# Norms in column form: x turned raw or scaled by its root on TensorE, factor and shift applied per partition

## The chip, the cores and the metric
One NeuronCore of a Trainium2 chip. The metric is the device time of one execution in microseconds (us); the kernel before had a median of 1973.52 us in 3 runs (1971.23 to 1974.72). Engines: PE (TensorE), DVE (VectorE), ACT (ScalarE), POOL (GpSimd), SP (SyncE). All data is fp32.

## The reference, cut to what matters
256 tokens of width 1024. Two transformer blocks, then two blocks that work on two streams, x and y (the context). Every stage begins with an RMS norm, a factor and a shift that depend on the condition c:

```python
h = rms_norm(x, norm1_g[i]) * (1.0 + sc1) + sh1      # rms_norm: x * rsqrt(mean(x*x) + eps) * g
x = x + g1 * attention(h)                            # i = 0 differential, i = 1 stick-breaking
h = rms_norm(x, norm2_g[i]) * (1.0 + sc2) + sh2
x = x + g2 * hierarchical_moe(h)                     # router: h @ w_group, h @ w_expert; 32 experts, top 2
```

The second pair of blocks does the same with one norm ahead of one wide input product. The matmuls contract over the width, so h is needed turned: 128 columns of the width on the partitions, 256 tokens along the row.

## The kernel before, in words
x lies as two tiles of 128 tokens x 1024. Six norms feed x: n = 0 to 3 (two for each of the first blocks, `transpose_h`, `take_hT`, `norm_tile`) and streams p = 1 and p = 3 (`stream_scale`, `stream_shift`, `turn_stream`, `take_turned`); p = 0 and 2 are the context's and stay. At each norm, for both tiles:

- ACT squares a tile with a sum and takes the root (L1436, L1438; L559, L560).
- DVE takes the reciprocal (L1602, L572), multiplies the tile with it and with the row `(1 + sc) * g` in one instruction (L1603, L573) and adds the row `sh` (L1604, L579). The rows hold the same 1024 numbers on all 128 partitions (`rows`), loaded by POOL as 512 KB broadcasts (L1286, L523, L530). In this step the columns are reordered from `(c k)` to `(k c)`, so x and the rows are read with a stride of 8 floats and h is written in order.
- PE turns the 8 chunks of the tile (L1918, L592; one weight load and one matmul each), idles through `keep_warm` matmuls (L584; each is two fp32 passes, so 8 of them are "x16" in the trace) and turns the second tile.
- ACT copies the turned chunks from PSUM to `hT` in four instructions of 512 (L1427). Then the first product starts. Matmuls of fp32 data are two instructions each, almost all recorded at the helper's line L1896.

The order of the work is written out by hand: every engine has its own list and waits on semaphores. PE carries, between its other work, 64 small products of the condition with `ada_w` and `w_mod` (`ada_item`), whose weights POOL loads into three buffers (L1295, `ada_load`); every 8 of them give rows of factors and shifts that DVE adds (L1582) and POOL stores to HBM and loads back when needed (`norm_load`, `norm_rows`). The large weights run on SP's queue through a ring of six 2 MB slots (L1230, L1251, L1254), a slot being loaded again when PE has used it.

For n = 0 the condition product comes first (eight 1 MB pieces of `ada_w`, t = 0 to 7, two `keep_warm` after each of t = 2 to 6), then its row is added (L1588), spread over partitions by PE (4 products with ones), and only then the norm is taken. After the norm n = 1 or 3 come the router's products, DVE's router chain (L1662 to L1723), the gathers of tokens for the first four experts, and the experts, each waiting for its weights. ACT's list in layer 1 has the context's squares (L559, once its load L1379 has landed, which POOL issues when h is done) between `take_hT(3)` and the two exponentials of the router.

Of the kernel before, what the change touches and what calls it, by code (L numbers as in the profile page):

```python
# [25 lines left out]
P = 128  # L26
# [34 lines left out]
COUNT.update({n: (4, 4, 4, 4) for n in ("h2T_mm", "h2T")})  # L61
# [71 lines left out]
def program(nc, a, out, sb, sem, ctx):  # L133
# [79 lines left out]
    lvec = small[:, 32:36]  # L213

# [115 lines left out]
    TURN = ((0, 1, 2, 3), (4, 5, 6, 0))  # L330
# [231 lines left out]
    def gain2(dve, link, p):  # L562

        dve.wait_ge(sem("rows2_in"), 16 * (3, 5, 8, 10)[p])
        link(nc.vector.scalar_tensor_tensor(rows[:, 0, :], rows[:, 0, :], 1.0, rows[:, 2, :], ALU.add, ALU.mult))

    def stream_scale(dve, link, p, t):
# [6 lines left out]
                                            rs2[:, k:k + 1], by_chunk(rows[:, 0, :]), ALU.mult, ALU.mult))  # L574

# [10 lines left out]
    def turn_stream(pe, p, ts, banks, spare=0, idle=(0, 0)):  # L586

        for i in range(TT):
            keep_warm(spare, idle[i])
            pe.wait_ge(sem("h2"), nth("h2", p, i + 1))  # L590
            for t in ts:
                ins = nc.tensor.transpose(bank[banks[(t - ts[0]) // 2]][:, (t % 2 * TT + i) * P:(t % 2 * TT + i + 1) * P],  # L592
                                          h2[p % 2][:, i, t * P:(t + 1) * P], ident)
                if i and t % 2:
                    ins.then_inc(sem("h2T_mm"), 1)

    def take_turned(act, copy, p, ts, banks):

        for t in ts[::2]:
            act.wait_ge(sem("h2T_mm"), nth("h2T_mm", p, t // 2 + 1))  # L600
            copy(hT2[:, t:t + 2, :], bank[banks[(t - ts[0]) // 2]].rearrange("p (t n) -> p t n", t=2)).then_inc(sem("h2T"), 1)

    def fill_mm(mm, p, n, halves, b):
# [112 lines left out]
    def act_second(act, link, copy):  # L716
# [115 lines left out]
        take_turned(act, copy, 3, range(KT), (0, 2, 4, 5))  # L832
# [17 lines left out]
    def dve_second(dve, link):  # L850
# [158 lines left out]
    def pe_second(pe, mm):  # L1009
# [163 lines left out]
        turn_stream(pe, 1, range(KT), (2, 3, 4, 5), 0, (22, 4))  # L1173
        pe.wait_ge(sem("h2T"), every("h2T", 1))
# [25 lines left out]
        turn_stream(pe, 3, range(KT), (0, 2, 4, 5), 3, (0, 13))  # L1200
        pe.wait_ge(sem("h2T"), every("h2T", 3))
# [14 lines left out]
    def _(sp):  # L1216
# [5 lines left out]
        def weight(l, n):  # L1222
# [3 lines left out]
            if n < 6:  # L1226
                src = W[:, n * 512:(n + 1) * 512].rearrange("(p t) n -> p t n", t=KT)
# [56 lines left out]
    def _(pool):  # L1284
# [34 lines left out]
        def norm_load(n):  # L1319
# [27 lines left out]
        row_load(3, a["norm1_g"][0:1, :].to_broadcast((P, D)), "norm_in")  # L1347
# [3 lines left out]
        pool.wait_ge(sem("first_mm"), 4)  # L1351
# [73 lines left out]
    def _(act):  # L1425
# [51 lines left out]
        def take_gathered(l, c, b):  # L1477

            act.wait_ge(sem("gat_mm"), EACH["gat_mm"] * l + c + 1)
            i = c % QUAD  # L1480
            copy(hS[:, c // QUAD % 2, 2 * i:2 * i + 2, 0:QUAD * LIST],
                 bank[b].rearrange("p (t n) -> p t n", t=2)[:, :, 0:QUAD * LIST]).then_inc(sem("hS"), 1)
# [8 lines left out]
        def overflow(l):  # L1491

            o_pe, o_act_done = sem(f"over_pe{l}"), sem(f"over_act{l}")
            for step in range(NX * NOVER):
                act.wait_ge(o_pe, 5 * step + 1)
                copy(o_selT.rearrange("p t n -> p (t n)"), bank[2][:, 0:S]).then_inc(o_act_done, 1)
                copy(o_h.rearrange("p t n -> p (t n)"), bank[4]).then_inc(o_act_done, 1)
# [41 lines left out]
        for l in range(2):  # L1539
# [18 lines left out]
            take_hT(2 * l + 1)  # L1558
# [15 lines left out]
    def _(dve):  # L1574
# [8 lines left out]

        def first_norm():

            dve.wait_ge(free(3), 1)
            dve.wait_ge(sem("first_bias"), 16)
            V.tensor_tensor(line, bank[7], line, ALU.add).then_inc(sem("first_line"), 1)  # L1588
            dve.wait_ge(sem("norm_in"), 16)
            dve.wait_ge(sem("first_mm"), 2)  # L1590
            link(V.scalar_tensor_tensor(rows[:, 0, :], psum[:, 4:6, :].rearrange("p b n -> p (b n)"), 1.0, rows[:, 3, :],
                                        ALU.add, ALU.mult))
            dve.wait_ge(sem("first_mm"), 4)
            for t in range(TT):
                norm_tile(0, t, psum[:, 6:8, :].rearrange("p b n -> p (b n)"))

        def norm_tile(n, t, shift):

            by_chunk = lambda r: r.rearrange("p (c k) -> p k c", k=KT)
            h_ = h[:, t, :].rearrange("p (k c) -> p k c", k=KT)  # L1600
            dve.wait_ge(sem("rms"), TT * n + t + 1)
            link(V.reciprocal(rstd[:, t:t + 1], ss[:, t:t + 1]))  # L1602
            link(V.scalar_tensor_tensor(h_, by_chunk(x[:, t, :]), rstd[:, t:t + 1], by_chunk(rows[:, 0, :]), ALU.mult, ALU.mult))  # L1603
# [650 lines left out]
```

## Time and profile before
| | before |
|---|---|
| median of 3 runs | 1973.52 us |
| profiled execution: its own time / its span | 1969.06 / 1967.2 us |
| granted clock of PE, mean | 0.962 |
| busy: PE / DVE / ACT / POOL | 1747.5 / 467.5 / 360.6 / 93.2 us |
| chain that ended last, by engine | PE 56%, DMA 29%, DVE 8%, ACT 3% |
| HBM read | 580.17 MB |

A busy PE is 89% of the span, `keep_warm` included (59.2 us of it). "Idle before, releaser" says how long an engine stood still ahead of an instruction and whose event ended that. A wait counts only where it lies on the chain that ends last.

### The profile page before, as it was taken

The numbers are of one execution on the slowest core, as the hardware profiler recorded it, in microseconds if no ns is written. First come the engines' busy times: TensorE is split into PE (matmuls) and PEld (weight loads), VectorE is DVE, ScalarE is ACT, GpSimd is POOL, SyncE is SP. The second block draws the span as 40 slices with busy tenths as digits, with TensorE's granted clock in tenths as the row PEclk, the third lists the DMA queues.
The fourth block names the chain that finished last, engine by engine and source line by source line (L and its number), as shares of the span: only waits on it lengthen the run. The fifth ranks groups of instructions, "written<-read, shape, count | busy, mean of one in ns | idle before, by whom it ended". The sixth has DMA issues, their size and how long they took to land.

```text
span 1967.2 us, 18627 instructions
## 1 busy us (share of the span) xinstructions
PE 1747.5 (89%) x7717; PEld 868.1 (44%) x7717; DVE 467.5 (24%) x908; ACT 360.6 (18%) x784; POOL 93.2 (5%) x165
## 2 busy tenths in 40 slices
PE   5996799888898887998999999999998899989988
PEld 2742353333333333654463433333343456555564
DVE  2006540000000102102342000000112434664363
ACT  1003210000001000104321010000000334352351
POOL 1012000000000010113100000000001000000000
PEclk9998899999999998999999999999999999999999
DMA  9988249999999999868349999999999522133220
GB/s 354 375 308 331 86 157 422 423 421 421 424 422 424 420 420 405 306 256 338 129 161 422 420 419 422 418 422 416 419 420 412 222 86 100 46 103 125 98 75 22
DMA packets 121640, 593.67 MB, mean 302 GB/s; under 512 B 9652, under 2 KB 14844, under 8 KB 96968
## 3 DMA queue, kind: packets, MB, share of 16 engines
q1 hardware_dynamic: 96680, 491.93, 61.9%
q0 software_dynamic: 17696, 89.40, 12.2%
q10 hardware_dynamic: 7168, 11.02, 1.5%
q8 instruction: 65, 1.06, 0.2%
q14 instruction: 31, 0.25, 0.0%
HBM read 580.17 MB, written 12.15 MB: 301 GB/s over the span
## 4 chain that ended last, share of the span: by engine, by line
PE 56%; DMA 29%; DVE 8%; ACT 3%; issue 3%; SPq 1%; POOL 1%; ACTq 0%; DVEq 0%
PE psum L1896 53%; DMA ring<-in_expert_w_up 22%; DMA ring<-in_expert_w_gate 2%; DMA work<-in_ada_w 2%; DMA ring<-in_ada_w 1%; ACT work L1427 1%; DMA ring<-in_w_out 1%; DVE small L922 1%; DVE work L1603 1%; PE psum L584 1%; PE psum L1055 1%; DVE work L1604 1%; DVE work L573 1%; DVE work L579 1%; PE psum L2095 0%
## 5 line engine op out<-in xcount | busy, mean ns | idle before, releaser
L1896 PE MATMUL psum<-ring,work 128*64 128x512 f32 (+5 forms) x4480 | 1165.6, 576 | 95.4 <-DMA ring<-in_expert_w_up 75.2
L1896 PEld LDWEIGHTS psum<-ring,work 128*64 128x64 f32 (+2 forms) x4480 | 449.7, 153 | 728.1 <-issue 697.6
L1896 PE MATMUL psum<-work 128*128 128x192 f32 (+7 forms) x880 | 184.4, 368 | 8.6 <-ACT work L1427 3.0
L1785 DVE TENSOR_TENSOR work<-work,psum 128x256 f32<-128x256 f32 x64 | 27.0, 422 | 630.0 <-ACT work L1528 630.0
L1896 PEld LDWEIGHTS psum<-work 128*128 128x128 f32 (+2 forms) x880 | 128.8, 196 | 99.0 <-issue 73.3
L1427 ACT ACTIVATE work<-psum 128x256 f32<-128x256 f32 (+5 forms) x241 | 113.6, 484 | 315.5 <-PE psum L1896 103.3
L1896 PE MATMUL psum<-work,ring 128*128 128x256 f32 (+1 forms) x728 | 161.9, 380 | 4.4 <-ACT work L1427 3.0
L1528 ACT ACTIVATE work<-psum 128x256 f32<-128x256 f32 x64 | 24.6, 385 | 727.8 <-PE psum L1896 727.8
L1896 PEld LDWEIGHTS psum<-work,ring 128*128 128x128 f32 x728 | 136.0, 191 | 35.0 <-issue 12.3
L1807 DVE TENSOR_TENSOR work<-psum,rows 128x512 f32<-128x512 f32 x64 | 44.2, 691 | 272.3 <-PE psum L1896 272.3
L1896 PE MATMUL psum<-work,small 128*1 128x512 f32 (+1 forms) x512 | 70.8, 642 | 14.6 <-DMA work<-in_ada_w 8.9
L1427 ACT ACTIVATE ring<-psum 128x512 f32<-128x512 f32 (+3 forms) x82 | 49.9, 609 | 75.2 <-PE psum L1896 54.9
L584 PE MATMUL psum<-cst 128*128 128x256 f32 x238 | 59.2, 404 | 0.0
L1582 DVE TENSOR_TENSOR rows<-psum,rows 128x512 f32<-128x512 f32 x8 | 5.5, 689 | 205.3 <-PE psum L1896 205.3
L584 PEld LDWEIGHTS psum<-cst 128*128 128x128 f32 x238 | 47.0, 203 | 15.3 <-issue 8.9
L1389 POOL DMA_INDIRECT work<-expert_rows,picks x8 | 7.7, 966 | 887.5 <-DMA expert_rows<-work 885.6
L2095 PE MATMUL psum<-cst,work 128*128 128x128 f32 x128 | 28.0, 300 | 16.4 <-DVE work L1785 16.4
L922 DVE TENSOR_REDUCE small<-psum 128x1 f32<-128x512 f32 (+1 forms) x48 | 28.7, 599 | 48.9 <-PE psum L1896 48.0
L1135 PE MATMUL psum<-cst,ring 128*128 128x128 f32 x160 | 27.6, 288 | 11.7 <-DVE ring L928 11.2
L795 ACT ACTIVATE ring<-psum,small 128x512 f32<-128x512 f32 (+1 forms) x48 | 29.6, 617 | 43.2 <-DVE small L922 41.7
L1135 PEld LDWEIGHTS psum<-cst,ring 128*128 128x128 f32 x160 | 19.4, 145 | 35.0 <-DVE ring L928 26.2
L1295 POOL DMA_DIRECT2D work<-in_ada_w x40 | 21.4, 538 | 258.7 <-PE psum L1896 258.7
(236 smaller groups left out, 798.3 us busy)
## 6 DMA issues: line engine op xcount, KB each, us to landing
ring<-in_expert_w_gate SPq DMA_DIRECT2D x64, 2048.0 KB, 17.5
ring<-in_expert_w_up SPq DMA_DIRECT2D x64, 2048.0 KB, 21.5
ring<-in_expert_w_down SPq DMA_DIRECT2D x64, 2048.0 KB, 21.2
work<-in_ada_w POOLq DMA_DIRECT2D x40, 1024.0 KB, 8.9
ring<-in_w_in SPq DMA_DIRECT2D x12, 2048.0 KB, 9.3
work<-in_w_mod POOLq DMA_DIRECT2D x16, 1024.0 KB, 5.2
ring<-in_diff_w_in SPq DMA_DIRECT2D x6, 2048.0 KB, 31.6
ring<-in_sb_w_in SPq DMA_DIRECT2D x6, 2048.0 KB, 22.2
```

The source lines that it names most:

```text
L573: link(nc.vector.scalar_tensor_tensor(h2[p % 2][:, t, :].rearrange("p (k c) -> p k c", k=KT), by_chunk(stream(p)[:, t, :]), rs2[:, k:k + 1 ...
L584: nc.tensor.matmul(bank[b][:, 0:S], ident, cst[:, 0:S], start=True, stop=True, skip_group_check=True)
L795: nc.scalar.activation(pe_[:, k % 3, 0:n * P], bank[4 + k % 3][:, 0:n * P], ACT.Exp, bias=nm2[:, k % 3:k % 3 + 1], accum_out=sm2[:, k % 4: ...
L922: V.tensor_reduce(nm2[:, k % 3:k % 3 + 1], bank[4 + k % 3][:, 0:n * P], AX.X, ALU.max, negate=True).then_inc(sem("a_max"), 1)
L1135: ins = T.transpose(bank[(7, 2)[u % 2]][:, j * P:(j + 1) * P], pe_[:, u % 3, j * P:(j + 1) * P], ident)
L1295: pool.dma_start(ada_in[:, i % 3, 512 * k:512 * (k + n)], src[:, c * 512:(c + n) * 512].rearrange("(p t) n -> p t n", t=KT)[:, t, :]).then ...
L1427: copy = lambda o_, i_: nc.scalar.activation(o_, i_, ACT.Copy)
L1528: nc.scalar.activation(s_act, gu_bank(e)[:, 0:S], ACT.Silu).then_inc(sem("silu"), 1)
L1785: V.tensor_tensor(hid, s_act, gu_bank(e)[:, S:2 * S], ALU.mult).then_inc(sem("hid"), 1)
L1807: V.tensor_tensor(outb[:, e % 2, :], bank[5 + e % 2], gate2, ALU.mult).then_inc(sem("out_ev"), 1)
L1896: return T.matmul(out_, lhsT, rhs, start=start, stop=stop, skip_group_check=True)
L2095: ins = T.transpose(bank[2][:, j * P:(j + 1) * P], src[:, j * P:(j + 1) * P], ident)
```

## The change
For the six norms of x:

- Factor and shift are no longer rows but columns: `col_set` holds for each norm three tiles of 128 x 8, loaded as 4 KB each (32 bytes for each partition). For n = 0 they are made on the chip: the added row is turned by four PE transposes and copied out by three small DVE instructions.
- n = 0, 2 and p = 1, 3: DVE makes `ident * rstd` (128 x 128) for each tile, and PE multiplies the raw chunk of x (as stationary operand, read with a stride of 8 floats except for n = 0) with it: a product of two instructions where a transpose is one. For n = 0 this stands between t = 5 and t = 6 of the condition product.
- n = 1, 3: PE turns raw x straight away, chunks read with the stride. DVE copies them out of PSUM (4 x 512). The factor is folded into the router's weights and the shift into its bias (`router_prep`, ahead of `update_x`, with one product with ones after the first of the four projection products), and the root is applied to the logits. Behind that ACT writes `x * rstd` to h (`scale_rows`), from which the experts' tokens are gathered; factor and shift are applied when they are evicted.
- ACT evicts one chunk (256 columns) at a time with scale and bias per partition, eight instructions in place of four, and the first product waits chunk by chunk.
- `keep_warm` counts: n = 0 from 9 + 4 to 5 (and the two after t = 5 go), between the tiles n = 1, 2, 3 from 8, 4, 9 to 8, 2, 8; the 15 ahead of n = 2 stay; p = 1 from 22 + 4 to 15 + 2; p = 3 from 13 to 5.

```diff
@@ norm_load(n)  (POOL)
-            row_load(0, mod[r + 1:r + 2, :].to_broadcast((P, D)), "norm_in")
-            row_load(1, mod[r:r + 1, :].to_broadcast((P, D)), "norm_in")
-            row_load(3, a["norm2_g" if half else "norm1_g"][l:l + 1, :].to_broadcast((P, D)), "norm_in")
+            for dst, src in zip(col_set[n], (mod[r + 1:r + 2, :], mod[r:r + 1, :], a["norm2_g" if half else "norm1_g"][l:l + 1, :])):
+                pool.dma_start(dst, src.rearrange("a (p t) -> p (a t)", p=P)).then_inc(sem("norm_in"), 16)
@@ ACT
+        def take_hT(n):
...
+            for t in range(KT):
+                if t % 2 == 0:
+                    act.wait_ge(sem("hT_mm"), 4 * n + t // 2 + 1)
+                nc.scalar.activation(hT[:, t, :], bank[TURN[0][t // 2]][:, t % 2 * S:(t % 2 + 1) * S], ACT.Identity,
+                                     scale=gain[:, t:t + 1], bias=shift[:, t:t + 1]).then_inc(sem("hT_done"), 1)
+        def scale_rows(n):
+            act.wait_ge(sem("hT_done"), HT_AT[n] + 4)
+            for t in range(TT):
+                nc.scalar.activation(h[:, t, :].rearrange("p (k c) -> p k c", k=KT), x[:, t, :].rearrange("p (c k) -> p k c", k=KT),
+                                     ACT.Copy, scale=rstd[:, t:t + 1]).then_inc(sem("h_done"), 1)
@@ DVE
+        def diag(n, t):
+            dve.wait_ge(sem("rms"), TT * n + t + 1)
+            link(V.reciprocal(rstd[:, t:t + 1], ss[:, t:t + 1]))
+            V.tensor_scalar(h[:, t, 0:P], ident, rstd[:, t:t + 1], None, ALU.mult).then_inc(sem("h_done"), 1)
+        def router_prep(l):
...
+            link(V.tensor_tensor(part, r_w, of_chunk(shift), ALU.mult))
+            V.tensor_reduce(kT[:, 2, 0:NG + NX], part.rearrange("p t n -> p n t"), AX.X, ALU.add).then_inc(sem("r_bias"), 1)
+            link(V.tensor_tensor(r_w, r_w, of_chunk(gain), ALU.mult))
+            dve.wait_ge(sem("r_bias"), 2 * l + 2)
+            link(V.tensor_tensor(r_b, r_b, bank[5][:, 0:NG + NX], ALU.add))
@@ update_x (DVE), after the last tile
+            for j in range(4):
+                dve.wait_ge(sem("hT_mm"), 4 * (n + 1) + j + 1)
+                if j == 3:
+                    dve.wait_ge(sem("rms"), TT * (n + 1) + TT)
+                    link(V.reciprocal(rstd, ss))
+                V.tensor_copy(hT[:, 2 * j:2 * j + 2, :], bank[TURN[1][j]].rearrange("p (t s) -> p t s", t=2)).then_inc(
+                    sem("hT_done"), 1)
@@ transpose_h(n)  (PE)
+                if tile and n:
+                    keep_warm((1, 2, 1)[n - 1], (8, 2, 8)[n - 1])
+                if n % 2:
+                    pe.wait_ge(sem("x_done" if tile else "x_half"), n)
...
+                    chunk = x[:, tile, t:D:KT] if n else x[:, tile, t * P:(t + 1) * P]
+                    if n % 2:
+                        ins = T.transpose(dst, chunk, ident)
+                    else:
+                        ins = mm(dst, chunk, h[:, tile, 0:P], True, True)
@@ the first work of PE
+            if t == 5:
+                transpose_h(0)
+            elif 1 < t < KT - 1:
                 keep_warm(0, 2)
         pe.wait_ge(sem("first_line"), 1)
-        for b, k in ((4, 2), (5, 3), (6, 0), (7, 1)):
-            mm(bank[b], C["ones"][32 * k:32 * k + 1, :], line[32 * k:32 * k + 1, :], True, True).then_inc(sem("first_mm"), 1)
+        for i in range(4):
+            ins = T.transpose(bank[2][:, i * P:(i + 1) * P], line[:, i * P:(i + 1) * P], ident)
+        ins.then_inc(sem("first_mm"), 1)
+        keep_warm(0, 5)
@@ streams p = 1 and 3 (turn_stream, take_turned and fill_mm change in the same way)
-        turn_stream(pe, 1, range(KT), (2, 3, 4, 5), 0, (22, 4))
+        turn_stream(pe, 1, range(KT), (2, 3, 4, 5), 0, (15, 2))
-        turn_stream(pe, 3, range(KT), (0, 2, 4, 5), 3, (0, 13))
+        turn_stream(pe, 3, range(KT), (2, 3, 4, 5), 0, (0, 5))
```

## Rows read from the trace of the kernel before

**Rows 1.** Chain that ended last: start us, us, what; one piece.
```profile
6.99 27.50 DMA ring<-in_ada_w
```
**Rows 2.** Stretches: length, busy (instructions) by engine, PEclk, DMA share, GB/s.
```profile
80.00:100.00 20.00, 19.85 (x103) 15.11 (x96) 0.00 (x0) 1.20 (x3) 1.59 (x3) 1.00 1.01 377
100.00:113.00 13.00, 12.85 (x67) 9.46 (x69) 0.00 (x0) 1.19 (x2) 0.53 (x1) 1.00 0.62 238
...
167.00:178.00 11.00, 5.81 (x42) 2.52 (x38) 7.73 (x21) 3.65 (x15) 1.86 (x4) 0.97 0.96 345
...
400.00:700.00 300.00, 261.82 (x1136) 103.46 (x1134) 26.95 (x52) 24.98 (x60) 0.00 (x0) 0.94 1.02 423
```
**Rows 3.** Timeline of PE, first norm: start us, us, instructions [idle before <-releaser].
```profile
29.59 1.04 PE L1896 MATMUL psum<-ring,small 128*1 128x512 f32 x8
...
48.65 3.72 PE L1896 MATMUL psum<-work,ring 128*128 128x256 f32 x16 [1.50 <-ACT work L1427]
```
**Rows 4.** Timeline of PE: pace of transposes and small products.
```profile
261.51 1.09 PE L1918 MATMUL psum<-cst,work 128*128 128x128 f32 x8 [0.51 <-DVE work L1604]
264.10 4.93 PE L1896 MATMUL psum<-work 128*128 128x36 f32 x32 [1.50 <-ACT work L1427]
```
**Rows 5.** ACT by shape: count, busy us, mean ns, idle before, releasers.
```profile
L795 ACT ACTIVATE ring<-psum,small 128x256 f32<-128x256 f32 x16 | 7.6, 474 | 14.3 <-DVE small L922 13.9
```
**Rows 6.** Line 1604 alone: ns min/median/max, first and last start.
```profile
L1604 DVE TENSOR_TENSOR work<-work,rows x6: 2009/2023/2030, 245.7 to 997.7; 128x1024 f32<-128x1024 f32 x6
L1604 DVE TENSOR_TENSOR work<-work,psum x2: 1221/1221/1221, 41.3 to 44.8; 128x1024 f32<-128x1024 f32 x2
```
**Rows 7.** Timelines of POOL and PE in the attentions of both layers.
```profile
164.57 1.07 POOL L1286 DMA_DIRECT2D rows<-mod_scratch x2
...
178.42 1.88 PE L1896 MATMUL psum<-work,small 128*1 128x512 f32 x8 [4.71 <-DMA work<-in_ada_w]
...
924.36 1.04 PE L1896 MATMUL psum<-work,small 128*2 128x512 f32 x8 [1.83 <-DMA work<-in_w_mod]
```
**Rows 8.** DMA issues, 0 to 12 us: tile, count, KB each, median us to landing.
```profile
ring<-in_diff_w_in SPq DMA_DIRECT2D x2, 2048.0 KB, 37.3
...
small<-in_c SPq DMA_DIRECT2D x2, 4.0 KB, 1.8
```
**Rows 9.** Timeline of DVE and PE at the norm n = 1.
```profile
254.29 1.23 DVE L1623 TENSOR_TENSOR x<-x,work 128x1024 f32<-128x1024 f32 x1
...
257.38 3.62 PE L584 MATMUL psum<-cst 128*128 128x256 f32 x16
```
**Rows 10.** Timeline of PE at the norm n = 2.
```profile
780.70 6.74 PE L584 MATMUL psum<-cst 128*128 128x256 f32 x30
788.76 2.76 PE L1896 MATMUL psum<-work,small 128*1 128x512 f32 x24 [1.32 <-DVE x L1752]
...
797.34 2.86 PE L1896 MATMUL psum<-work,ring 128*128 128x256 f32 x12 [1.50 <-ACT work L1427]
```
**Rows 11.** Timeline of POOL, ACT and PE at n = 3.
```profile
999.99 0.73 POOL L1379 DMA_DIRECT2D work<-in_ctx x1 [40.13 <-DVE work L1604]
...
1007.65 1.06 ACT L559 ACTIVATE work<-work 128x1024 f32<-128x1024 f32 x1 [5.36 <-DMA work<-in_ctx]
...
1016.68 5.47 PE L1896 MATMUL psum<-work 128*128 128x192 f32 x32 [0.98 <-DVE work L1723]
```
**Rows 12.** Timeline of PE and ACT at the streams p = 1 and p = 3.
```profile
1540.39 9.76 PE L584 MATMUL psum<-cst 128*128 128x256 f32 x44
1546.79 0.29 ACT L560 ACTIVATE small<-small 128x1 f32<-128x1 f32 x1
...
1558.12 7.13 PE L1896 MATMUL psum<-ring,work 128*128 128x512 f32 x16 [1.50 <-ACT work L1427]
...
1797.67 1.04 PE L592 MATMUL psum<-cst,work 128*128 128x128 f32 x8
...
1807.98 4.21 PE L1896 MATMUL psum<-ring,work 128*128 128x160 f32 x29 [1.50 <-ACT work L1427]
```

More of the change, by code:

```diff
@@ L213, in program @@
     lvec = small[:, 32:36]
+    col_set = [[small[:, at_ + 8 * k:at_ + 8 * k + 8] for k in range(3)] for at_ in (488, 368, 392, 416, 440, 464)]
+    HT_AT = (0, 8, 12, 20)
     carve = Carver(base)
@@ L600, in take_turned @@
             act.wait_ge(sem("h2T_mm"), nth("h2T_mm", p, t // 2 + 1))
+            if p % 2:
+                gain, shift, _ = col_set[4 + p // 2]
+                for k in (t, t + 1):
+                    nc.scalar.activation(hT2[:, k, :], bank[banks[t // 2]][:, k % 2 * S:(k % 2 + 1) * S], ACT.Identity,
+                                         scale=gain[:, k:k + 1], bias=shift[:, k:k + 1]).then_inc(sem("h2T"), 1)
+                continue
             copy(hT2[:, t:t + 2, :], bank[banks[(t - ts[0]) // 2]].rearrange("p (t n) -> p t n", t=2)).then_inc(sem("h2T"), 1)
@@ L831, in act_second @@
         stream_rms(act, link, 3, 1)
-        take_turned(act, copy, 3, range(KT), (0, 2, 4, 5))
+        take_turned(act, copy, 3, range(KT), (2, 3, 4, 5))
         for n, js in enumerate(X1_IN):
@@ L1440, in take_hT @@
         def take_hT(n):
-            for j in range(4):
-                act.wait_ge(sem("hT_mm"), 4 * n + j + 1)
-                copy(hT[:, 2 * j:2 * j + 2, :], bank[TURN[n % 2][j]].rearrange("p (t s) -> p t s", t=2)).then_inc(sem("hT_done"), 1)
+            gain, shift, _ = col_set[n]
+            if n == 0:
+                act.wait_ge(sem("first_line"), 2)
+            for t in range(KT):
[8 more added lines that the diff above has]
+                                     ACT.Copy, scale=rstd[:, t:t + 1]).then_inc(sem("h_done"), 1)
         def take_qkv(l):
@@ L1479, in take_gathered @@
             act.wait_ge(sem("gat_mm"), EACH["gat_mm"] * l + c + 1)
-            i = c % QUAD
-            copy(hS[:, c // QUAD % 2, 2 * i:2 * i + 2, 0:QUAD * LIST],
-                 bank[b].rearrange("p (t n) -> p t n", t=2)[:, :, 0:QUAD * LIST]).then_inc(sem("hS"), 1)
+            gain, shift, _ = col_set[2 * l + 1]
+            for k in range(2):
+                t = 2 * (c % QUAD) + k
+                ins = nc.scalar.activation(hS[:, c // QUAD % 2, t, 0:QUAD * LIST], bank[b][:, k * S:k * S + QUAD * LIST],
+                                           ACT.Identity, scale=gain[:, t:t + 1], bias=shift[:, t:t + 1])
+            ins.then_inc(sem("hS"), 1)
         def store(l, e):
@@ L1496, in overflow @@
                 copy(o_selT.rearrange("p t n -> p (t n)"), bank[2][:, 0:S]).then_inc(o_act_done, 1)
-                copy(o_h.rearrange("p t n -> p (t n)"), bank[4]).then_inc(o_act_done, 1)
+                gain, shift, _ = col_set[2 * l + 1]
+                for t in range(KT):
+                    ins = nc.scalar.activation(o_h[:, t, :], bank[4][:, t * SLOTS:(t + 1) * SLOTS], ACT.Identity,
+                                               scale=gain[:, t:t + 1], bias=shift[:, t:t + 1])
+                ins.then_inc(o_act_done, 1)
                 act.wait_ge(o_pe, 5 * step + 2)
@@ L1557, in _ @@
             square_norm(2 * l + 1)
-            take_hT(2 * l + 1)
+            scale_rows(2 * l + 1)
             if l:
@@ L1582, in ada_take @@
             V.tensor_tensor(line, bank[7], line, ALU.add).then_inc(sem("ada_row"), 1)
[L1584 to L1595, printed above, removed]
@@ L1608, in gain_row, with gain_cols @@
-        def gain_row(n):
-            dve.wait_ge(sem("norm_in"), 16 * (1 + 3 * n))
-            link(V.scalar_tensor_tensor(rows[:, 0, :], rows[:, 0, :], 1.0, rows[:, 3, :], ALU.add, ALU.mult))
+            V.tensor_scalar(h[:, t, 0:P], ident, rstd[:, t:t + 1], None, ALU.mult).then_inc(sem("h_done"), 1)
+        def gain_cols(n):
+            gain, _, g_ = col_set[n]
+            dve.wait_ge(sem("norm_in"), 48 * n)
+            link(V.scalar_tensor_tensor(gain, gain, 1.0, g_, ALU.add, ALU.mult))
@@ new lines, in first_norm @@
+        def first_norm():
+            dve.wait_ge(sem("consts"), 16)
+            for t in range(TT):
+                diag(0, t)
+            dve.wait_ge(free(3), 1)
+            dve.wait_ge(sem("first_bias"), 32)
+            V.tensor_tensor(line, bank[7], line, ALU.add).then_inc(sem("first_line"), 1)
+            dve.wait_ge(sem("first_mm"), 1)
+            turned = bank[2].rearrange("p (i k r) -> p i k r", i=4, k=4)
+            by_row = lambda t_: t_.rearrange("p (k i) -> p i k", k=2)
+            gain, shift, g_ = col_set[0]
+            link(V.tensor_copy(by_row(g_), turned[:, :, 0:2, 1]))
+            link(V.scalar_tensor_tensor(by_row(gain), turned[:, :, 2:4, 0], 1.0, by_row(g_), ALU.add, ALU.mult))
+            V.tensor_copy(by_row(shift), turned[:, :, 0:2, 0]).then_inc(sem("first_line"), 1)
@@ L1754, in combine @@
                 dve.wait_ge(sem("x_done" if t else "x_half"), n + 1)
-                if l == 0:
-                    norm_tile(n + 1, t, rows[:, 1, :])
+            if l == 0:
+                for t in range(TT):
+                    diag(n + 1, t)
         def overflow(l):
@@ L1875, in _ @@
                                                ALU.min, ALU.add).then_inc(sem("s_log"), 1)
+            router_prep(l)
             update_x(2 * l, "proj_mm", v)
```

105 lines of the change are left out of this document (58 added, 47 removed).

## The prediction, made blind
> **What bounds the kernel now.** I read the stretches first, then the chain, then the timelines of PE, POOL and ACT around each norm. The stretches fall into three kinds. In the expert stages the DMA engines are full (share 1.02, 423 GB/s) and PE waits for weights [rows 2]; what is saved inside them is worth nothing, but what is saved ahead of them moves the start of the loads and so the end. From 48 to about 120 us PE is full (19.85 of 20 us) while the DMA share is 1.01 as well, and falls to 0.62 in 100 to 113 us [rows 2]: two limits side by side. The norms themselves are gaps in the chain: the first product stands behind the load of `ada_w`, which ends at 34.5 us [rows 1], by 14 us, down to an ACT wait of 1.50 us [rows 3]. So every norm is on the path, and the question at each is what PE's list still holds when DVE's long instructions are gone.
>
> **Prices.** A small fp32 product costs 4.93/32 = 0.154 us for each instruction, a transpose 1.09/8 = 0.136 [rows 4], an idling pair 3.62/8 = 0.45 [rows 9]. A tile turned by products is 16 instructions, so 2.5 us where a transpose took 1.1. An ACT eviction of 256 columns with a column operand I take at 0.474 [rows 5], the shape nearest to it; 8 of them are 3.8 us, about PE's own pace for the eight chunks, so they are covered after the first. I take 0.6 us for DVE's copy of 512 out of PSUM (estimate, from half of the 1.22 of 1024 in rows 6), 0.2 for each small DVE step. The new 4 KB column loads are like `small<-in_c`, 1.8 us [rows 8], and each takes POOL the same 0.53 as the row load it replaces, one more for p = 1 and p = 3; their readers wait for 48 more later than before, with tens of us in between. Unknown is one thing: the stationary chunk of x is read with a stride of 8 floats, and no row shows PE doing that. From both sides: nothing, or what it costs DVE. There an add with one strided operand in SBUF took 2.02 us and with it in PSUM 1.22 [rows 6], 0.8 us for 1024 or 0.10 for 128 columns; a gain is excluded, since the same numbers are read. I take nothing, the value of the nearest rows of PE's own [rows 4], and keep 0.10 for the range.
>
> On this a rule bears that speaks against the change. The Trainium skill (Advanced Engine Details and Errata, SBUF Cachelines) says that SBUF lines have 16 bytes, that two accesses to a line are needed to hide its latency, and that another line for each access is paid for. By that rule every load of a strided chunk would be slower; DVE's 2.02 against 1.22 us agrees, and for PE no run here shows it.
>
> **Start, n = 0.** Removed: the 512 KB broadcast of g beside the first loads, 0.5 MB at the 377 to 400 GB/s of a full stretch [rows 2], about 1.2 us for everything in the queue. Added: 32 products of two tiles between t = 5 and t = 6, 5.0 us. t = 5 begins at 29.59 [rows 3], now 28.4, ends 29.4; the tiles end 34.4; t = 6, two idling pairs and t = 7 end 37.5. DVE's row 38.3, four transposes 38.9, three small copies 39.6, first eviction 40.1. PE has 5 idling pairs (2.25) behind the transposes: 41.2. Eviction paces with the products, so the first product begins at 41.2 instead of 48.65 [rows 3]: -7.4. The first two weights, issued before 12 us, land after 37.3 in the median [rows 8], so the second at about 50; it is needed 15.4 us after the start (two steps of 7.2 and an item), at 56.6: no wait. But loads of the condition's weights run with the DMA share at 1.01 until 100 us [rows 2]; the share of 0.62 behind holds 13 x 0.38 = 5 us of air, less than the shift. I charge 1 us for that: **-6.4**, bounds 0 and -7.4.
>
> **n = 1.** PE's list after the projections: three condition items, tile 0, 8 idling pairs that end at 261.0 [rows 9], tile 1 at 261.51 [rows 4]. Raw x of tile 1 is ready at 255.5 [rows 9], so DVE's chain is gone, but the 8 pairs stand where they stood: what is late next is `keep_warm`. Tile 1 begins at 261.0; DVE's copies run 261.4 to 264.0 with a reciprocal among them; the router's first tile keeps up, its second half (16 x 0.154 = 2.5) ends 267.1, against 264.10 + 4.93 = 269.0 [rows 4]. -1.9. DVE's four logit steps in place of two (+0.35) are beside PE's 18 idling instructions. The first four gathers now end with two evictions of 192 instead of one of 384, +0.2. `router_prep` lies under the last three projection products, `scale_rows` under the router chain. **-1.7** (strided, 16 transposes: -0.1).
>
> **n = 2.** 15 idling pairs end at 787.4, then the wait for x of 1.32, then items (2.76) [rows 10]. x, whose four adds of 0.7 begin at 780.0, is now ready at 782.9, so PE goes on at 787.4: items to 790.2, tile 0 to 792.7, 2 pairs 793.6, tile 1 796.1, product at once, against 797.34. **-1.2** (strided, 32 loads: +2.0).
>
> **n = 3.** PE's side alone would give about 3 us (8 pairs end at 998.4, logits at 1004.4 instead of 1008.2). But POOL issues the context's load when h is done, at 999.99 so far [rows 11]; h is now written by `scale_rows` behind the copies (1001.4), two ACT instructions of 1.06 each, 1003.6. The load landed 7.66 us after its issue, with weights in front of it that will be gone by then; I take 5.5 (bounds 4 and 7.7): 1009.3. ACT then has two squares with roots (2.9), a table load (1.28) and both exponentials, 1014.0; DVE 5 steps, place and pick: the gathers begin at 1015.9 instead of 1016.68 [rows 11]. **-0.7** (+1.5 if the landing stays and the stride costs ACT too). The wait that is removed from DVE comes back as one on the context.
>
> **Attention stages.** `norm_load(1)` puts three broadcasts, 1.5 MB (two of them shown), ahead of a piece of `ada_w`, for which PE waits 4.71 us at 178.42 [rows 7], in a stretch at share 0.96 and 345 GB/s [rows 2]. 1.5 MB are 4.5 us; I take **-4.0**, bounds 0 and -4.7. `norm_load(3)` is ahead of the wait of 1.83 at 924.36 [rows 7]: **-1.8**. `norm_load(2)` is issued while the ring stands still: nothing.
>
> **p = 1.** 22 idling pairs (9.76) [rows 12] become 15, 6.65: 1547.0. Both roots are there at 1547.1 [rows 12]. Tile 0 to 1549.6, 2 pairs 1550.5, tile 1 1553.0; before, the product began at 1558.12 [rows 12]: -5. Seven us later it needs the small weights of the front part, which land about when they did; I charge 1.1. **-3.9** (strided: -0.7). **p = 3.** Tile 0 from 1797.67 [rows 12] to 1800.2, 5 pairs 1802.4, tile 1 1805.0 against 1807.98 [rows 12]: **-3.0** (strided: +0.2).
>
> **Sum.** 6.4 + 1.7 + 1.2 + 0.7 + 4.0 + 1.8 + 3.9 + 3.0 = 22.7 us. The profiled execution took 1969.06 us: 1946.4. The median of the runs is 4.5 above it: 1950.9.
>
> **The rivals.**
> - *Strided weight loads.* 0.10 us for each: n = 1 16, n = 2 32, p = 1 32, p = 3 32 loads on the path, 11.2 us, and 2 at n = 3: 22.7 - 13.2 = 9.5, **1964.0**. For it: DVE's 2.02 against 1.22 [rows 6]. Against: a whole matmul stands on one read of the chunk, and DVE's surcharge is not there where its operand is in PSUM, so it is of one port and not of every reader. The other side begins here: each load on PE's path counts 112 times (n = 3 behind the context not counted), so from 22.7/112 = 0.20 us for each, twice DVE's surcharge, nothing is gained, and at 0.30 the time is 1973.5 + 11 = **1984**.
> - *The start's gain is lost to the DMA queue.* If the loads up to 178 us are the limit, the 7.4 us of n = 0 come back as waits for `ada_w`: **1957.3**. For it: share 1.01. Against: 0.62 in 100 to 113 us, and no PE wait of over 1.1 us ahead of 150.
> - *Idling pairs and the clock.* The change leaves pairs as the last work ahead of n = 1, 2, 3. If the products and transposes between them leave PE too quiet, the clock falls to 1.2 GHz ahead of a first product; six such dips at 1 to 2 us each (estimate: half of a tile's 2.5 or of the first 3.5 of products) are some 8: **1959**. For it: the mean of 1.00 in the stretches at PE's full work against 0.94 where it waits [rows 2].
> - *The change doesn't do what it says*: every reader still ends behind something else in its list, as at n = 1 and 3, at p = 1 and 3 too: 22.7 - 6.9 (p = 1 and 3) = 15.8, **1957.7**.
>
> **How the numbers follow.** Forecast 0.50, strided loads 0.22 and, dearer than DVE's, 0.08, queue 0.10, clock 0.05, something else first 0.05. The forecast's own range is 1945 to 1956. The range for 8 in 10 goes from 1942 (both attention waits and the whole start) to 1966, the strided case included. A change under 0.2% (3.9 us) can't be told from none here: faster means under 1969.6. Faster: all of 0.50, 0.20 of the strided 0.22, 0.01 of the dear 0.08 and 0.15 of the last three's 0.20, 0.86. Slower, over 1977.4: 0.05 of the dear; within: the rest, 0.09.
>
> **What would show it.** First product of layer 0 at 41 us; PE's 16 instructions of a tile in 2.5 us at n = 2 and p = 1, the strided loads as long as those of n = 0 (longer by 0.1: the first rival); tile 1 of n = 1 right behind 8 idling pairs; the wait at 178 gone or under 1 us; the exponentials of layer 1 released by the context's squares; more than 5 us of new waits on `in_ada_w` before 180 would show the queue. It is wrong if the sum of the first products' shifts at n = 2 and p = 1 is under 3 us.

## The result, and the profile after

The changed kernel takes 1954.9 us (median of 4 runs, 1950.8 to 1955.4) against 1974.1 (4 runs, 1971.2 to 1975.4): ratio 0.9895, 95% interval 0.9876 to 0.9914, so 19.2 us faster; forecast were 1950.9 and a range of 1942 to 1966. The profiled executions took 1969.06 (span 1967.2) and 1954.97 us (span 1953.1), only 14.1 apart: that of before lies 5 us below its median, that of after on it. The steps below are told profile to profile. They are less sharp than their decimals: over stretches where two kernels have the same instructions, their profiles differed by up to 3 us, mostly by how long PE ran at half clock there.

| | before | after |
|---|---|---|
| granted clock of PE, mean | 0.962 | 0.961 |
| busy: PE / DVE / ACT / POOL, us | 1747.5 / 467.5 / 360.6 / 93.2 | 1748.9 / 425.8 / 398.5 / 94.1 |
| `keep_warm`, us | 59.2 | 42.5 |
| HBM read, MB | 580.17 | 572.89 |
| chain: PE / DMA / DVE / ACT | 56 / 29 / 8 / 3% | 59 / 28 / 6 / 3% |

17 us of idling pairs are gone and PE is as busy as before: six strided tiles of products take some 2.75 us each more than transposes did, 16.5. The same landmark of PE's list, looked up in both traces, gives what each part moved (us after minus before, negative is earlier):

| part | forecast | moved | shift then |
|---|---|---|---|
| start, n = 0 | -6.4 | -7.4 | -7.4 |
| layer 0's attention (no broadcasts) | -4.0 | -6.3 | -13.7 |
| projection of layer 0 (clock) | 0 | +1.9 | -11.8 |
| n = 1, to the first gate/up | -1.7 | -0.8 | -12.6 |
| experts of layer 0 | 0 | +0.2 | -12.4 |
| n = 2 | -1.2 | +1.2 | -11.2 |
| layer 1's attention | -1.8 | -0.1 | -11.3 |
| projection and n = 3 | -0.7 | +3.7 | -7.6 |
| experts of layer 1 | 0 | -2.7 | -10.3 |
| p = 1, to `turn_c` | -3.9 | -0.7 | -11.0 |
| p = 3, with the 0.7 ahead of it | -3.0 | -1.5 | -12.5 |
| the rest | 0 | -1.6 | -14.1 |

PE's timeline at the start [rows 3]; columns as there:

```profile
29.61 1.04 PE L1959 MATMUL psum<-ring,small 128*1 128x512 f32 x8
30.58 3.84 PE L1959 MATMUL psum<-work,x 128*128 128x128 f32 x32
...
38.23 0.66 PE L2290 MATMUL psum<-cst,rows 128*128 128x128 f32 x4 [0.81 <-DVE rows L1647]
38.72 2.32 PE L602 MATMUL psum<-cst 128*128 128x256 f32 x10
41.27 1.99 PE L1959 MATMUL psum<-work,ring 128*128 128x256 f32 x8 [0.22 <-DMA ring<-in_diff_w_in]
```

Both tiles of products, x read contiguously, lie in 3.84 us: 0.12 for each instruction, not 0.154. The 0.154 came from a row whose stretch (264.10 to 269.03 us) had a granted clock of 0.74 in the mean; the same router products at full clock take 0.12. The piece of the condition product ahead of the tiles, t = 5, begins at 29.61, where it began before, and not at 28.4: taking the broadcast of g away moved nothing there. The first product stands at 41.27, as forecast, and waits for its weights by then, no longer for ACT. In layer 0's attention the wait of 4.71 us [rows 7] is down to these two:

```profile
166.00 1.04 PE L1959 MATMUL psum<-work,small 128*1 128x512 f32 x8 [0.91 <-DMA work<-in_ada_w]
...
168.49 1.04 PE L1959 MATMUL psum<-work,small 128*1 128x512 f32 x8 [0.44 <-DMA work<-in_ada_w]
```

PE at n = 1, to be held against [rows 4, 9]: the 8 pairs stand between the tiles, and tile 1 follows right behind them.

```profile
244.68 1.16 PE L1985 MATMUL psum<-cst,x 128*128 128x128 f32 x8
245.68 3.62 PE L602 MATMUL psum<-cst 128*128 128x256 f32 x16
249.13 1.05 PE L1985 MATMUL psum<-cst,x 128*128 128x128 f32 x8
```

PE at n = 2 [rows 10]; the same rows stand at p = 1 and p = 3 (3.84 to 3.87 us a tile) [rows 12]:

```profile
777.65 4.08 PE L1959 MATMUL psum<-work,x 128*128 128x128 f32 x16
781.57 1.03 PE L602 MATMUL psum<-cst 128*128 128x256 f32 x4
782.43 3.86 PE L1959 MATMUL psum<-work,x 128*128 128x128 f32 x16
```

A tile of 16 costs what 32 cost at the start: 0.24 us for each instruction. By line, with min/median/max in ns (PEld is the weight load): the product and then the transpose, both with strided x as stationary operand, and last the transposes of the context's streams, whose chunks are contiguous:

```profile
L612 PEld LDWEIGHTS psum<-work,x x64: 312/335/336, 1536.5 to 1795.1; 128*128 128x128 f32 x64
...
L1985 PEld LDWEIGHTS psum<-cst,x x32: 186/192/207, 244.7 to 987.9; 128*128 128x128 f32 x32
...
L615 PEld LDWEIGHTS psum<-cst,work x32: 138/141/143, 1053.2 to 1743.2; 128*128 128x128 f32 x32
```

The contiguous products of n = 0 load in a mean of 192 ns. So the stride costs the product's load 143 ns and the transpose's 51 ns: the 128 transposes of all the norms in the kernel before, contiguous too, loaded in 138 to 143 ns. What differs is what PE makes of it. Eight strided transposes took 1.05 to 1.16 us, as the contiguous ones did (1.04 to 1.09), each load lying under its neighbours; the strided products took twice the time of the contiguous ones.

POOL, ACT and PE at n = 3 [rows 11], three timelines:

```profile
994.91 0.72 POOL L1403 DMA_DIRECT2D work<-in_ctx  x1 [46.35 <-ACT work L1479]
```

```profile
990.42 4.21 ACT L1479 ACTIVATE work<-x,small 128x1024 f32<-128x1024 f32 x2 [6.22 <-DVE work L1685]
1000.15 1.06 ACT L566 ACTIVATE work<-work 128x1024 f32<-128x1024 f32 x1 [5.53 <-DMA work<-in_ctx]
...
1004.30 0.21 ACT L1607 ACTIVATE work<-work 128x8 f32<-128x8 f32 x1
```

```profile
999.40 1.30 PE L1959 MATMUL psum<-work,cst 128*128 128x32 f32 x10 [1.29 <-DVE work L1753]
1006.58 7.52 PE L1959 MATMUL psum<-work 128*128 128x192 f32 x32 [5.88 <-DVE work L1785]
1015.10 1.08 PE L1959 MATMUL psum<-ring,work 128*64 128x512 f32 x4 [1.00 <-ACT work L1520]
```

To be read upwards: gathers behind the exponentials, these behind the context's squares, these behind its load, that behind `scale_rows`, which takes ACT 2.1 us a tile. Its input has the stride, its output is in order; ACT's squares of as many contiguous numbers take 1.06. Then the p = 1 wait, at PE's `turn_c` (the transposes behind the first wide product), and the DVE step that it stands behind:

```profile
1554.09 0.66 PE L1052 MATMUL psum<-cst,ring 128*128 128x128 f32 x4 [2.11 <-DVE work L704]
```

```profile
1552.16 0.18 DVE L699 RECIPROCAL small<-small 128x4 f32<-128x4 f32 x1 [14.85 <-DMA ring<-in_consts]
```

### The profile page after: what moved, and what is told of

It reads as the page before. It is cut to its first block, busy times and chain, and to the rows that moved or that the text cites. A ratio compares the mean times of both kernels' runs of the same rounds, so it can differ in the third digit from the quotient of the medians.

```text
span 1953.1 us, 18724 instructions
## 1 busy us (share of the span) xinstructions
PE 1748.9 (90%) x7721; PEld 876.1 (45%) x7721; DVE 425.8 (22%) x912; ACT 398.5 (20%) x860; POOL 94.1 (5%) x167
## 3 DMA queue, kind: packets, MB, share of 16 engines
HBM read 572.89 MB, written 12.15 MB: 300 GB/s over the span
## 4 chain that ended last, share of the span: by engine, by line
PE 59%; DMA 28%; DVE 6%; ACT 3%; issue 3%; SPq 1%; ACTq 0%; DVEq 0%
PE psum L1959 55%; DMA ring<-in_expert_w_up 21%; DMA ring<-in_expert_w_gate 2%; DMA ring<-in_diff_w_in 2%; DMA work<-in_ada_w 1%; PE psum L602 1%; DVE small L952 1%; SPq L481 1%; DMA ring<-in_consts 1%; PE psum L1082 1%; PE psum L2169 1%; DVE work L1848 0%; ACT work L1572 0%; DVE work L1927 0%; DMA ring<-in_w_out 0%
## 5 line engine op out<-in xcount | busy, mean ns | idle before, releaser
L1959 PE MATMUL psum<-work 128*128 128x192 f32 (+7 forms) x880 | 185.0, 367 | 11.5 <-DVE work L1785 6.9
L1451 ACT ACTIVATE work<-psum 128x256 f32<-128x256 f32 (+4 forms) x153 | 69.7, 461 | 237.6 <-PE psum L1959 73.7
L1520 ACT ACTIVATE work<-psum,small 128x192 f32<-128x192 f32 x128 | 58.4, 506 | 25.0 <-PE psum L1959 25.0
L602 PE MATMUL psum<-cst 128*128 128x256 f32 x178 | 42.5, 390 | 0.0
L602 PEld LDWEIGHTS psum<-cst 128*128 128x128 f32 x178 | 33.4, 194 | 11.6 <-issue 7.5
L1162 PE MATMUL psum<-cst,ring 128*128 128x128 f32 x160 | 27.4, 287 | 11.9 <-DVE ring L958 11.3
```

What stands on the lines that cost most here:

```text
L602: nc.tensor.matmul(bank[b][:, 0:S], ident, cst[:, 0:S], start=True, stop=True, skip_group_check=True)
L1162: ins = T.transpose(bank[(7, 2)[u % 2]][:, j * P:(j + 1) * P], pe_[:, u % 3, j * P:(j + 1) * P], ident)
L1451: copy = lambda o_, i_: nc.scalar.activation(o_, i_, ACT.Copy)
L1520: ins = nc.scalar.activation(hS[:, c // QUAD % 2, t, 0:QUAD * LIST], bank[b][:, k * S:k * S + QUAD * LIST], ACT.Identity, scale=gain[:, t: ...
L1959: return T.matmul(out_, lhsT, rhs, start=start, stop=stop, skip_group_check=True)
```

## The experiments

Theory after the comparison: start and missing broadcasts make the gain; what the other norms win on DVE is paid back in strided weight loads (n = 2, p = 1, p = 3), in the late context load (n = 3), in pads that were left (n = 1, 2, 3), and at p = 1 in the wait for the small weights. Rivals: the queue eats the start, and the clock is the cause. Each kernel is the changed one with one edit, up to the last two, which join several. "Profile" is the span against 1953.1; ratios are to the kernel before, run beside it (medians of 1972.7 to 1976.4 us).

**Contiguous chunks.**

```diff
-chunk = x[:, tile, t:D:KT] if n else x[:, tile, t * P:(t + 1) * P]
+chunk = x[:, tile, t:D:KT] if n % 2 else x[:, tile, t * P:(t + 1) * P]
-matmul(dst, stream(p)[:, i, t:D:KT], h2[p % 2][:, i, 0:P], ...)
+matmul(dst, stream(p)[:, i, t * P:(t + 1) * P], h2[p % 2][:, i, 0:P], ...)
```

> The products at n = 2, p = 1 and p = 3 read contiguous chunks of x as their stationary operand in place of chunks with a stride of 8 floats (leaves out the right order of the columns, so the output is not the reference's). Stride theory: the 16 products of a tile take 1.9 us in place of 3.85, as at n = 0; n = 2 gains 3.8 us and p = 3 gains 3.8, p = 1 gains 3.8 at its first product but hands it to the wait for the small weights; end -7.6 us against the changed kernel, 1947. Rival, fp32 products with a 128-wide diagonal are slow there for another reason (the clock, where x lies, the eviction's pace): tiles stay at 3.85 and the end moves by less than 1 us.

Measured 1950.8 us, ratio 0.9880 (0.9837 to 0.9923), profile -8.5. Two tiles of PE, n = 2 and p = 3:

```profile
776.40 2.05 PE L1959 MATMUL psum<-work,x 128*128 128x128 f32 x16
...
1779.07 1.95 PE L612 MATMUL psum<-work,x 128*128 128x128 f32 x16
...
1548.23 1.11 PE L1052 MATMUL psum<-cst,ring 128*128 128x128 f32 x4 [5.56 <-DVE work L704]
```

Their loads, at the lines of p = 1 and 3:

```profile
L612 PEld LDWEIGHTS psum<-work,x x64: 186/192/192, 1531.0 to 1784.6; 128*128 128x128 f32 x64
```

The stride theory holds to a tenth: against the changed kernel's PE list n = 2 gives 3.9, p = 3 3.8, p = 1 3.8 at the product, and the last of the PE rows shows that p = 1 hands it on as a wait of 5.56 in place of 2.11. By medians it is 4 us, with intervals that overlap; the mechanism rests on the rows.

**Row broadcasts back.**

```diff
 for dst, src in zip(col_set[n], ...): pool.dma_start(...)
+row_load(0, mod[r + 1:r + 2, :].to_broadcast((P, D)), "extra_in")
+row_load(1, mod[r:r + 1, :].to_broadcast((P, D)), "extra_in")
+row_load(3, a["norm2_g" if half else "norm1_g"][l:l + 1, :].to_broadcast((P, D)), "extra_in")
```

> The changed kernel, with the three 512 KB broadcasts of a norm loaded again at n = 1, 2 and 3 behind the small column loads, read by nobody. DMA theory: PE's waits for ada_w between 160 and 200 us come back and the layer-0 projection starts 6.3 us later; at n = 3 another 0 to 1.8; end +6 to +8 us, 1962. Rival, the shift there grew for another reason (the 7.4 us of the start put the pieces elsewhere, or the clock): under +1.5 us.

Measured 1965.2 us, ratio 0.9958 (0.9940 to 0.9976), profile +11.1. PE in both attentions:

```profile
170.65 1.89 PE L1965 MATMUL psum<-work,small 128*1 128x512 f32 x8 [5.55 <-DMA work<-in_ada_w]
...
920.08 1.89 PE L1965 MATMUL psum<-work,small 128*2 128x512 f32 x8 [4.69 <-DMA work<-in_w_mod]
```

Both waits are back, and the shift grows from 0 to +5.5 at the first and from +5.7 to +10.9 at the second, more than the 0 to 1.8 expected there. The second wait has PE at half clock right behind it (a product of the condition takes 1.89 us in place of 1.04), which is part of its price. Just ahead of it the shift had fallen to +2.8, for the changed kernel's profile has a longer stretch at half clock there; counted from that, the price is 8.1. By medians 10.3 us of 19.2 are loads that nobody needed at this size; by the ratios it is 12.4 of 20.7.

**A later start.**

```diff
-keep_warm(0, 5)
+keep_warm(0, 21)
```

> The changed kernel with 16 more idling pairs ahead of layer 0's first product, 16 x 0.45 = 7.2 us, about what the new start gained. If the start's gain goes through to the end: first product +7.2 at 48.5 us, end +7.2, 1962. Rival, the loads of the condition's weights are the limit up to 178 us and would have met a later start as well: waits for ada_w shrink by as much and the end moves by at most +2.

Measured 1962.2 us, ratio 0.9933 (0.9911 to 0.9954): +7.3, profile +9.5. The first product came at 46.64, not 48.5, in part because PE's list ahead of the pads ran 0.9 to 1.6 us earlier in this run. So the first product is only 5.4 us later than in the changed kernel; the shift is 6.7 us at the first gate/up of layer 0, behind all the waits for `ada_w`, and 9.4 at the end. Nothing of a later start is absorbed, and the queue rival falls.

**The context's load earlier.**

```diff
-pool.wait_ge(sem("h_done"), TT * 4)
+pool.wait_ge(sem("x_done"), 3)
 pool.dma_start(y_raw, a["ctx_2"]...)
```

> The context's load in layer 1 waits for x after the projection in place of h from the scaled rows. Theory that this load gates the router of n = 3: it is issued about 4.5 us earlier, PE's idle 5.9 us ahead of the gathers shrinks to about 1, first gate/up -4 to -6 us; by the end of the experts, whose loads are the limit, about half is left: end -2 to -3, 1952. Rival, the landing time depends on the weights in front and not on the issue: first gate/up moves by under 1 us, end 0.

Measured 1947.4 us, ratio 0.9862 (0.9819 to 0.9905), profile -7.5. PE ahead of the first gate/up:

```profile
996.58 1.30 PE L1959 MATMUL psum<-work,cst 128*128 128x32 f32 x10
998.95 7.12 PE L1959 MATMUL psum<-work 128*128 128x192 f32 x32 [1.07 <-DVE work L1785]
1007.07 2.37 PE L1959 MATMUL psum<-ring,work 128*64 128x512 f32 x10 [1.00 <-ACT work L1520]
```

5.88 of wait became 1.07. The first gate/up is 8.0 us earlier, but 4.7 of it stood ahead of n = 3 already, where nothing was edited: single profiles differ by that much there (2.9 of it in layer 1's attention, told below). At n = 3 itself it is 3.3, after a router at half clock (4.29 us in place of 2.42) took 1.9 back. So the edit is worth 3.3 us by the rows, less than the 7.5 of the medians. The experts kept nearly all of the 8.0 to the end (7.5), against my "half".

**Scaled copy and transposes.**

```diff
-V.tensor_scalar(h[:, t, 0:P], ident, rstd[:, t:t + 1], None, ALU.mult)        # n = 2; n = 0 stays
+V.tensor_scalar(h[:, t, :], x[:, t, :], rstd[:, t:t + 1], None, ALU.mult)
-ins = mm(dst, x[:, tile, t:D:KT], h[:, tile, 0:P], True, True)
+ins = T.transpose(dst, h[:, tile, t:D:KT], ident)
 # p = 1, 3 alike, with h2 and rs2
```

> At n = 2, p = 1 and p = 3 the vector engine writes x times its root (1024 columns, contiguous, one instruction of about 0.7 to 1 us) and TensorE transposes that copy with the same stride of 8, in place of a product of strided x with a diagonal. Theory (the stride is dear for the product's weight load only, the transposes of n = 1 and 3 took 1.1 us a tile from strided x): a tile goes from 3.85 to 1.1 us; n = 2 gains 5.4, p = 3 3 to 5 (tile 2 then waits for its copy), p = 1 5 at its first product, lost to the wait for the small weights; end -8 to -10 us, 1946. Rival (the copy on VectorE is what the change took off the path, and comes back): n = 2 and p = 3 gain under 2 each, end -3 or less.

Measured 1949.0 us, ratio 0.9865 (0.9837 to 0.9894), profile -6.5. PE at n = 2 and p = 3:

```profile
777.74 1.15 PE L1985 MATMUL psum<-cst,work 128*128 128x128 f32 x8
...
1783.83 1.16 PE L612 MATMUL psum<-cst,work 128*128 128x128 f32 x8 [1.15 <-DVE work L592]
...
1545.38 1.11 PE L1051 MATMUL psum<-cst,ring 128*128 128x128 f32 x4 [6.75 <-DVE work L703]
```

1.05 to 1.15 us a tile from a strided copy, at 189 ns for each weight load of p = 1 and 3; DVE's contiguous copy took 0.75. n = 2 gave 5.3. p = 1 gained 5.4 at its product and kept 0.7 of it behind the wait (6.75). p = 3 gave 4.0, and lost 1.15 to the copy, which starts late because ACT's root stands behind an eviction.

**Bytes out of p = 1's way.**

```diff
 pool.wait_ge(sem("h2"), every("h2", 1))
+pool.wait_ge(sem("c_n"), nth("c_n", 0, TT))
 norm_rows(pool, 2)
```

> The three 512 KB row broadcasts of norm p = 2 are issued behind c_norm of p = 0 in place of ahead of it. Theory (the small weights' landing is the limit of p = 1, and these 1.5 MB share the queue with them): the last small load lands up to 3.7 us earlier, TensorE's wait of 2.11 at turn_c goes, end -2 us, 1953. Rival (the issuing of many small loads is the limit, not bytes): the landing stays within 1 us and the end with it.

Measured 1951.8 us, ratio 0.9877 (0.9849 to 0.9904): -3.1. DVE's first step, which waits for the last small load, and PE:

```profile
1547.83 0.18 DVE L700 RECIPROCAL small<-small 128x4 f32<-128x4 f32 x1 [11.88 <-DMA ring<-in_consts]
```

```profile
1543.58 7.03 PE L1960 MATMUL psum<-ring,work 128*128 128x512 f32 x16
1550.44 0.60 PE L1053 MATMUL psum<-cst,ring 128*128 128x128 f32 x4
```

Landing 4.3 earlier, 3.0 of it against the p = 1 product, and no wait at PE.

**Fewer pads.**

```diff
-keep_warm((1, 2, 1)[n - 1], (8, 2, 8)[n - 1])
+keep_warm((1, 2, 1)[n - 1], (0, 2, 0)[n - 1])
-keep_warm(2, 15)
+keep_warm(2, 5)
```

> The idling pairs that were left between the tiles of n = 1 and n = 3 go (8 to 0 in both), 15 ahead of n = 2 become 5. Theory (they are what is late after the change): tile 2 of n = 1 and n = 3 begins 3.6 us earlier, the items of n = 2 4.2 us earlier; n = 3 passes nothing on, its router waits for the context's squares; sum -3.6 - 4.2 = -8, 1947, if the clock stays. Rival (clock): with PE quieter ahead of the routers the granted clock falls to 1.2 GHz for one stretch more at each, 3.4 us at half speed is 1.7 us back for each, and what is left is -3.

Measured 1945.3 us, ratio 0.9841 (0.9812 to 0.9870): -9.6, the largest gain of a single edit. In PE's list n = 1 gained 3.5, n = 2 4.3 and n = 3 3.5 at its second tile. The profile as a whole moved by -7.5 only, for it stood 6.2 us late ahead of n = 1, where nothing is edited. At n = 3 PE ran at half clock: 24 pad instructions that were left took 7.10 us in place of 5.43, ahead of a wait of 4.38:

```profile
986.68 7.10 PE L602 MATMUL psum<-cst 128*128 128x256 f32 x24
...
999.19 7.67 PE L1959 MATMUL psum<-work 128*128 128x192 f32 x32 [4.38 <-DVE work L1785]
```

That looks like the clock rival, but these pads took 6.88 us as well in the runs with the later start and the earlier context, which have all their pads, and the router in front of them ran at full clock (2.42 us) in both kernels below, where the same pads are gone. So no run shows a price for trimming.

**All four together**: the context's load, the scaled copy, the bytes at p = 1 and the pads in one kernel.

> All four edits together: the scaled copy with transposes, the context's load behind x, the row broadcasts of p = 2 behind c_norm, the trimmed idling pairs. If they add up: 8 to 10 from the copies (and up to 3 of p = 1 that the small weights' wait took), 7 from the context's load, 2 from the row broadcasts, 8 and 3.6 more at n = 3 from the pairs; -29 us at most, 1926; with the expert stages' weight loads taking back a third of what is won ahead of them: 1933.

Measured 1931.1 us, ratio 0.9781 (0.9758 to 0.9804), 2.2% below before and 23.8 below the changed kernel. Two waits are left, at n = 3 and p = 1:

```profile
985.04 8.47 PE L1960 MATMUL psum<-work 128*128 128x192 f32 x32 [4.05 <-DVE work L1786]
...
1528.21 1.11 PE L1052 MATMUL psum<-cst,ring 128*128 128x128 f32 x4 [3.63 <-DVE work L704]
```

**Both waits attacked**, on top of all four.

```diff
 # ACT, layer 1: stream_rms(0, t) from ahead of the exponentials to behind the first four gather evictions
 # ACT: stream_rms(3, 1) ahead of take_unit(2, 1)
 # small weights: consts2 first on SyncE, the five row broadcasts from GpSimd
-keep_warm(0, (9, 12)[l])
+keep_warm(0, (3, 12)[l])
```

> The version with all four edits, and four more: the squares and roots of the context go behind layer 1's first gather evictions (under the first gate/up product of 7.1 us) and no longer stand ahead of the router's exponentials; the small row weights of the front part are issued by GpSimd beside SyncE's, the constants ahead of the other small weights; the root of p = 3's second tile ahead of an eviction; 9 idling pairs ahead of layer 0's rank products become 3. Theory, each on the path: 4.0 for the exponentials' wait at n = 3, 3.6 for the wait at turn_c of p = 1, 1.1 at p = 3, 2.5 at n = 1: -11, 1920. Rival, the waits are handed on (the first gathers to the gate/up weights, which at layer 1 then are what is late, and turn_c to the last matrix of the small weights): half of it, 1926.

Measured 1929.6 us, ratio 0.9772 (0.9742 to 0.9802): not to be told from the one before. PE at the same two places:

```profile
986.57 5.44 PE L1970 MATMUL psum<-work 128*128 128x192 f32 x32 [1.07 <-DVE work L1796]
...
1527.99 1.11 PE L1060 MATMUL psum<-cst,ring 128*128 128x128 f32 x4 [3.46 <-DVE work L712]
```

At n = 3 the wait is gone and the first gate/up comes 5.9 us earlier than the attention ahead of it would have it, but layer 1's experts end where they did (1506.04 against 1506.09 us): here they wait for weights. At p = 1 the last issue went from 1517.5 to 1511.1 us and the landing from 1526.28 to 1526.07: the issuing is not the limit there, and the run above points to the bytes in the queue.

## Why the prediction was right, and where it was not

The time and its sign were right; the way to it was right in the first half only, and that the sum came out is luck. Two runs split the 19.2 us: 7.3 are the start, 10.3 the broadcasts, and what is left for the five norms n = 1 to 3, p = 1 and p = 3 together is 1.6 (by the ratios 0.8), less than the intervals can tell from nothing, where I had 10.5. Each of the three figures is a difference of medians that is itself sure to some 6 us only. The table has the same: n = 1 to 3, p = 1 and p = 3 moved by +1.9 in sum (the 2.7 that layer 1's experts gave back not counted). The prediction's own sign says so too: it was to be wrong if the first products of n = 2 and p = 1 moved by under 3 us together. Each against the shift ahead of it, they moved by +1.2 and -2.9, 1.7 us earlier in all.

- **Start** (-6.4): -7.4. The first product at 41.27 agrees with my 41.2 because two errors cancel: the 1.2 us for the broadcast of g did not come (t = 5 at 29.61, not 28.4), and the 32 products took 3.84 us, 1.2 less than my 5.0. The 1 us charged for the queue was not taken, and the second weight did not wait.
- **Broadcasts** (-4.0 and -1.8): mis-sized. Putting them back costs 5.5 and 5.1. I bounded each by the wait of before, in a kernel whose PE came 7 us later to that place; a wait shows only what the work ahead of it did not hide, so it was no upper bound for the earlier kernel. In layer 1 the changed kernel's profile showed no gain: the 1.83 went, but a longer stretch at half clock had taken 1.3 ahead of it, and a DVE wait of 0.91 where 0.45 had been took 0.5 behind it. Much of that is this one profile: its clock is 0.89 in the mean of 878 to 925 us, and 0.96 in four later runs with the same attention, which came 2.9 to 3.1 us earlier out of it.
- **Strided weight loads** (taken as nothing, kept at 0.10 as a rival with 0.22): this step failed. Measured 0.12 us for each instruction of a product (0.24 against 0.12), 96 of them, 11.5 us of PE; against the 0.154 that my sum used it is 0.09. My argument against it, that a matmul stands on one read of the chunk, was no price. n = 2 moved by +1.2 (strided rival: +2.0), p = 1 by -0.7 (-0.7, though most of that is the wait for the small weights), p = 3 by -0.8 (+0.2). The Trainium skill's rule (Advanced Engine Details and Errata, SBUF Cachelines) had the sign. The traces agree for both uses of the chunk: a product's load took 335 ns against 192, a transpose's 192 against 141. But the transposes of n = 1 and 3 still took 1.05 to 1.16 us a tile, as before.
- **n = 1** (-1.7): -0.8. `keep_warm` was late next, as said, and the router began 1.9 earlier, as forecast. Its second part ran at a mean clock of 0.59 (3.87 us, where the same 20 instructions took 2.42 at n = 3), which took 0.8 back, and the first gate/up waits 1.00 us for two evictions of 192 columns (0.58 for one before).
- **n = 3** (-0.7): +3.5 of the +3.7. The chain was the one that I wrote, and the landing took 5.2, near the 5.5 that I took. The mis-sized term is `scale_rows`, 4.2 us where I had 2.1: its input is strided, and that ACT pays for the stride too is the likely reason, but no run has it contiguous. Then 5.88 us of PE standing still were followed by gathers at half clock, 7.52 in place of 5.44.
- **p = 1** (-3.9): -0.7, for the stride (the product came 2.9 earlier, not 5) and then for the small weights: I charged 1.1 for them, and they held the gain to 0.7 however early the product came (0.7 of 5.4 in the scaled copy's run).
- **Clock**: the mean stayed (0.962, 0.961). Half-speed stretches moved rather than multiplied: the projection of layer 0 (27.7 to 29.7 us) and n = 3 lost to them. The dips of this rival did come at the router of n = 1 and the gathers of n = 3, but no run ties them to the pads.

The 8.6 us by which the profiles fall short of the sum did not show in the medians in full, because the profiled run of before lay 5 us low. A right number stood on terms of the start and the broadcasts that were too small (12.2 together, 17.6 measured) and five terms of the other norms that were too large (10.5, 1.6 measured). The last 1.6 us of the table, behind p = 3, had no term and no experiment.

Open: why the same strided chunk adds 143 ns to a product's load and 51 ns to a transpose's, and why only the first slows PE down. The traces show both prices and no cause.

## What to carry to other kernels

Price a moved operation for the engine that gets it, with its access pattern: a DVE or ACT surcharge for a stride is a warning for PE, and a contiguous scaled copy (0.75 us) plus transposes beat the product from strided data. When a chain is shortened, look at once for what else is released by its last step (a DMA two stages on) and what the idle padding around it still holds; here trimming pads (9.6 us) gave more than the arithmetic of five norms (1.6). Broadcasting a row to all partitions through a busy DMA queue can cost more than the instructions that use it; loads put back as dummies show their price, where the wait in the trace of before showed a part of it.

## What the runs showed of the hardware

- A product whose 128x128 fp32 stationary operand has a stride of 8 floats: 335 ns for each weight load against 192 contiguous; 3.85 us for 16 instructions against 1.95. Transposes with the same operand: 192 ns against 141 contiguous, with no more time for a tile (1.05 to 1.16 us for 8).
- ACT over 128x1024, a copy with a strided input and a scale for each partition: 2.1 us. ACT's square with a sum over 128x1024 contiguous: 1.06.
- The context's 1 MB load took 5.2 us from issue to landing when issued at 994.9, 10.6 at 978.3 and 11.9 at 966.7 (three kernels).
- PE's granted clock falls to half in stretches whose place and length vary from one profile to the next where the instructions are the same: 0.89 against 0.96 in the mean of one 47 us stretch, 3 us of time.
